# Steps reordered where the stages of a two-block transformer kernel meet

## The reference

```python
h = rmsnorm(x, g_pre_mix);  proj = h @ w_in          # u | x,B,C | q,k,v | f | 3 gates
y_a = s5_mixer(u, ...);  y_b = B * conv3(C * x);  y_c = forgetting_attention(q, k, v, f)
merged = sum(sigmoid(gate_b + bias_b) * (y_b @ w_branch_b) for b in 3 branches)
x = x + rmsnorm(merged @ w_out, g_post_mix)
x = x + rmsnorm(relu(rmsnorm(x, g_pre_mlp) @ w_ff1) ** 2 @ w_ff2, g_post_mlp)
```

```python
h = rmsnorm(x, norm1_g);  proj = h @ w_in_2          # q,k,v of 3 dilations | u,v | 2 gates
merged = sigmoid(gate_a) * (attn @ w_proj_attn) + sigmoid(gate_b) * (sgu @ w_proj_sgu)
x = x + merged @ w_out_2
h = rmsnorm(x, norm2_g);  x = x + (silu(h @ w_ffn_gate) * (h @ w_ffn_up)) @ w_ffn_down
out = rmsnorm(x, final_g)
```

## Time and profile before

| | before |
|---|---|
| median of 3 runs, us | 3589.28 (3587.01 to 3590.35) |
| the profiled execution, us | 3586.24 |
| its span, us | 3584.4 |
| TensorE busy, us (share) | 3479.1 (97%) |
| VectorE busy | 1387.6 (39%) |
| GpSimd busy | 967.8 (27%) |
| ScalarE busy | 941.1 (26%) |
| mean granted TensorE clock, of full | 0.989 |

### The profile page before, as it was taken

One profiled execution on the slowest core, in us unless ns is written; L12 is line 12 of the kernel. 1 busy time (PEld: TensorE's weight loads), 2 busy tenths in 40 slices (PEclk: granted clock), 3 DMA queues, 4 the chain that ended last, 5 costly groups with the idle time before them and its releaser, 6 DMA issues.

```text
span 3584.4 us, 44185 instructions
## 1 busy us (share of the span) xinstructions
PE 3479.1 (97%) x17275; PEld 2873.2 (80%) x17275; DVE 1387.6 (39%) x2452; ACT 941.1 (26%) x1575; POOL 967.8 (27%) x421
## 2 busy tenths in 40 slices
PE   7899999999999999999999999998999999999999
PEld 6688877888877888888778888887788888888887
DVE  6883443123335333333643444335124312232234
ACT  4223434322242111111433333332322211111112
POOL 1552102232215333333212222221322132222321
PEclk9999999999999999999999999999999999999999
DMA  4233012212312111111221212213123111111111
GB/s 131 62 76 95 22 54 65 70 53 65 123 53 83 47 48 56 48 47 47 71 86 47 66 53 59 78 42 115 53 65 111 36 60 52 47 47 47 47 47 59
DMA packets 203976, 226.83 MB, mean 63 GB/s; under 512 B 19224, under 2 KB 177604, under 8 KB 203340
## 3 DMA queue, kind: packets, MB, share of 16 engines
q1 hardware_dynamic: 178556, 169.85, 15.4%
q10 hardware_dynamic: 20912, 44.54, 3.6%
q0 software_dynamic: 4384, 10.74, 0.9%
HBM read 191.30 MB, written 31.69 MB: 62 GB/s over the span
## 4 chain that ended last, share of the span: by engine, by line
PE 87%; DVE 4%; issue 4%; ACT 2%; POOL 1%; DMA 1%; ACTq 0%; DVEq 0%; POOLq 0%
PE ps L274 18%; PE ps L319 16%; PE ps L301 13%; PE ps L302 13%; PE ps L295 13%; PE ps L770 4%; PE ps L2838 2%; PE ps L2809 1%; POOL wlo L266 1%; PE ps L2826 1%; PE ps L2321 1%; PE ps L336 1%; PE ps L510 1%; ACT whi L258 1%; PE ps L2302 1%
## 5 line engine op out<-in xcount | busy, mean ns | idle before, releaser
L266 POOL TENSOR_TENSOR wlo<-raw,whi 128x2048 fp32r<-128x2048 f32 (+1 forms) x162 | 699.4, 4318 | 1731.1 <-ACT whi L258 1730.2
L301 PE MATMUL ps<-h_lo,whi 128*128 128x512 f32 x1856 | 723.8, 390 | 2.0 <-POOL wlo L266 2.0
L302 PE MATMUL ps<-h_hi,wlo 128*128 128x512 f32 x1856 | 723.5, 390 | 0.0
L258 ACT ACTIVATE whi<-raw 128x2048 fp32r<-128x2048 f32 (+1 forms) x162 | 288.1, 1779 | 883.1 <-PE ps L295 595.9
L295 PE MATMUL ps<-h_hi,whi 128*128 128x512 f32 x1856 | 461.6, 391 | 5.0 <-issue 2.7
L295 PEld LDWEIGHTS ps<-h_hi,whi 128*128 128x128 f32 x1856 | 349.2, 188 | 79.0 <-issue 5.8
L301 PEld LDWEIGHTS ps<-h_lo,whi 128*128 128x128 f32 x1856 | 349.5, 188 | 75.7 <-POOL wlo L266 3.1
L302 PEld LDWEIGHTS ps<-h_hi,wlo 128*128 128x128 f32 x1856 | 349.3, 188 | 72.6
L1157 DVE TENSOR_TENSOR big<-big,ps 128x512 f32<-128x512 f32 x400 | 274.4, 687 | 240.3 <-PE ps L274 240.2
L319 PE MATMUL ps<-h_lo,whi 128*128 128x512 f32 x880 | 352.2, 400 | 2.0 <-POOL wlo L266 1.9
L319 PE MATMUL ps<-h_hi,wlo 128*128 128x512 f32 x880 | 344.8, 392 | 0.0
(11 more groups left out here) (335 smaller groups left out, 4817.8 us busy)
## 6 DMA issues: line engine op xcount, KB each, us to landing
raw<-in_w_ff_dram SPq DMA_DIRECT2D x32, 1024.0 KB, 5.2
raw<-in_w_in_dram SPq DMA_DIRECT2D x57, 512.0 KB, 4.6
raw<-in_w_in_dram SPq DMA_DIRECT2D x28, 1024.0 KB, 5.3
raw<-in_w_ffn_gate_dram SPq DMA_DIRECT2D x11, 1024.0 KB, 5.3
raw<-in_w_ffn_up_dram SPq DMA_DIRECT2D x11, 1024.0 KB, 5.3
raw<-in_w_ffn_down_dram SPq DMA_DIRECT2D x11, 1024.0 KB, 4.9
yt<-y_keep ACTq DMA_DIRECT2D x20, 512.0 KB, 3.9
raw<-in_w_out_dram SPq DMA_DIRECT2D x8, 1024.0 KB, 5.0
```

Of the source, the lines that this page charges most:

```text
L258: nc.scalar.activation(whi[c % 2][:, 0:cols], raw[c % 2][:, 0:cols], ACT.Copy).then_inc(s_hi.sem, 1)
L266: nc.gpsimd.tensor_tensor(wlo[c % 2][:, 0:cols], raw[c % 2][:, 0:cols], whi[c % 2][:, 0:cols].bitcast(F32), ALU.subtract).then_inc(s_lo.se ...
L301: nc.tensor.matmul(ps[:, bank + n, :], w(0, k, m * P, P), src[1][:, k, sl], start=False, stop=False)
L302: last = nc.tensor.matmul(ps[:, bank + n, :], w(1, k, m * P, P), src[0][:, k, sl], start=False, stop=k == ks - 1)
```

## The change

Nothing is computed otherwise but for the squarings of S5; steps are put at other places, and each engine's part of a stage is changed to fit.

- *First norm (Start).* ScalarE issues the loads of x pairs 2 and 3 after pair 0 has landed. All four stood first before.
- *Output projections (Out).* `turn` of features 0 to 7 of half 0 stands behind tiles (2,6), (2,7), (3,4) and (3,5), two at each, in place of (2,4) to (2,7). The hi split of the feed-forward's first unit stands amid the features of half 0, that of its second ahead of the features of half 1.
- *Merges.* The first branch's quarters of y are loaded at once, the last two into `gate`, on two more semaphores, and the split of the first branch unit is put ahead of y's. In the loop, the split of the next branch unit stands behind the sigmoids and the split of the next gate unit; it stood ahead of the sigmoids.
- *Feed-forward's last pair.* `dve_norm` ahead of `dve_post`; features 0 to 3 of half 0 ahead of the last rows' sums and of the unit split on ScalarE; turns behind parts 13 and 15 of pass 0 and parts 12 and 13 of pass 1.
- *S5's first round.* VectorE makes round 0's last doubling itself (`first_half`); `taps` ahead of the kernel rows and `by_b(0, 0)` ahead of the scans; a squaring takes four operations in place of six; TensorE does round 1's first two half tiles ahead of `outputs(0)`.
- *Dilated attention's first pass.* `features` ahead of the exponentials.
- *Gate stage.* The eleven loads of `wsp`, `lng`, `lnb` and `bsp` go from ScalarE's queue to SyncE's, behind the first two units.

```diff
-                for q in range(4):
+                def load(q):
                     e.dma_start(big[:, 2 * q:2 * q + 2, :],
                                 A["x"][0, 2 * q * P:(2 * q + 2) * P, :].rearrange("(t p) d -> p t d", p=P)
                                 ).then_inc(x_pair[q].sem, 16)
+                load(0)
+                load(1)
                 e.wait_ge(eps_set.sem, 1)
                 nc.scalar.activation(nst[:, RP, 0:1], eps_c[:, :], ACT.Sqrt)
                 r = self.rows
+                e.wait_ge(x_pair[0].sem, 16)
+                load(2)
+                load(3)
                 for t in range(8):
                     r.act_pre(e, t)
...
                     if g == 0:
-                        self.rows.act_features(e, 0)
-                        split_hi(e, unit_no(self.u + 4))
+                        for k in range(8):
+                            if k == 4:
+                                split_hi(e, unit_no(self.u + 4))
+                            self.rows.act_hi(e, 0, k)
                 if self.gain is not None:
                     e.wait_ge(x_rows.sem, self.rows.x + 8)
                     e.dma_start(scratch["x_keep"], big[:, :, :]).then_inc(d_out.sem, 16)
+                split_hi(e, unit_no(self.u + 5))
...
                                 e.wait_ge(dve_a.sem, self.da + t + 1)
                             tile(j, t, t == 0 if j == 2 else t == 4)
-                            if g == 1 and j == 2:
-                                for k in range(2 * t - 8, 2 * t - 6):
-                                    self.rows.turn(e, 0, k)
+                            k = {(2, 6): 0, (2, 7): 2, (3, 4): 4, (3, 5): 6}.get((j, t))
+                            if k is not None:
+                                self.rows.turn(e, 0, k)
+                                self.rows.turn(e, 0, k + 1)
...
-                self.i = (d_in.take(32 * nb), d_in2.take(32 * nb))
+                self.i = (d_in.take(32 * nb - 16), d_in2.take(32 * nb - 16))
+                self.i2, self.i3 = d_tab.take(16), d_gain.take(16)
...
+            def place(b, k):
+                return gate[:, 2 * k - 4:2 * k - 2, :].rearrange("p a n -> p (a n)") if b == 0 and k >= 2 else yt[:, k % 2, :]
+            def wait_y(self, e, b, k):
+                if b == 0 and k >= 2:
+                    e.wait_ge((d_tab, d_gain)[k % 2].sem, (self.i2, self.i3)[k % 2] + 16)
+                else:
+                    e.wait_ge((d_in, d_in2)[k % 2].sem, self.i[k % 2] + 16 * ((4 * b + k) // 2 + (1 if b == 0 else 0)))
...
             def act(self, e):
                 self.begin(e)
+                for k in range(4):
+                    e.dma_start(self.place(0, k), scratch["y_keep"][0, :, k, :]).then_inc((d_in, d_in2, d_tab, d_gain)[k].sem, 16)
+                split_hi(e, unit_no(self.u + 1))
+                for k in range(4):
+                    self.wait_y(e, 0, k)
+                    nc.scalar.activation(y_hi[:, k, :], self.place(0, k), ACT.Copy).then_inc(ac.sem, 1)
+                def gates(b, i):
...
+                    split_hi(e, unit_no(self.u + 8 * b + 2, i))
                 for b in range(self.nb):
-                    for k in range(4):
-                        n = 4 * b + k
-                        if n >= 2:
-                            e.wait_ge(dve_a.sem, self.lo + n - 1)
-                        e.dma_start(yt[:, k % 2, :], scratch["y_keep"][b, :, k, :]).then_inc((d_in, d_in2)[k % 2].sem, 16)
-                        if k == 0:
-                            continue
-                        if k == 1 and b:
-                            e.wait_ge(pe_b.sem, self.b + 16 * b)
-                        for kk in (0, 1) if k == 1 else (k,):
-                            e.wait_ge((d_in, d_in2)[kk % 2].sem, self.i[kk % 2] + 16 * ((4 * b + kk) // 2 + 1))
-                            nc.scalar.activation(y_hi[:, kk, :], yt[:, kk % 2, :], ACT.Copy).then_inc(ac.sem, 1)
-                    with e.Fori(0, 4) as i:
-                        if self.bias is not None:
-                            e.wait_ge(act_a.sem, 4 * i + (self.aa + 16 * b))
...
-                        split_hi(e, unit_no(self.u + 8 * b + 1, i))
-                        for n in range(4):
...
-                        split_hi(e, unit_no(self.u + 8 * b + 2, i))
+                    if b:
+                        for k in range(4):
+                            e.wait_ge(dve_a.sem, self.lo + (4 * b + k - 1 if b > 1 or k > 1 else 4))
+                            e.dma_start(yt[:, k % 2, :], scratch["y_keep"][b, :, k, :]).then_inc((d_in, d_in2)[k % 2].sem, 16)
+                            if k == 0:
+                                continue
+                            if k == 1:
+                                e.wait_ge(pe_b.sem, self.b + 16 * b)
+                            for kk in (0, 1) if k == 1 else (k,):
+                                self.wait_y(e, b, kk)
+                                nc.scalar.activation(y_hi[:, kk, :], yt[:, kk % 2, :], ACT.Copy).then_inc(ac.sem, 1)
+                    else:
+                        e.wait_ge(dve_a.sem, self.lo + 4)
+                    if b:
+                        split_hi(e, unit_no(self.u + 8 * b + 1))
+                    with e.Fori(0, 3) as i:
+                        gates(b, i)
+                        split_hi(e, unit_no(self.u + 8 * b + 3, i))
+                    gates(b, 3)
...
-                        nc.vector.tensor_tensor(y_lo[:, k, :], yt[:, k % 2, :], y_hi[:, k, :].bitcast(F32),
+                        nc.vector.tensor_tensor(y_lo[:, k, :], self.place(b, k), y_hi[:, k, :].bitcast(F32),
...
                 e.dma_start(gpb[:, :], self.gain.partition_broadcast(P)).then_inc(d_gain.sem, 16)
                 def ups(c, i, us):
-                    split_hi(e, (us[0][0] + 1,) + us[0][1:])
+                    if not (i is None and c == 0):
+                        split_hi(e, (us[0][0] + 1,) + us[0][1:])
                     for n in range(4):
                         if not (i is None and c == 0):
...
                         summed(t)
                         r.act_post(e, t)
-                        if t:
+                        if 0 < t < 5:
                             r.act_pre(e, t - 1)
+                    r.act_pre(e, 4)
+                    for k in range(2):
+                        r.act_hi(e, 0, k)
                     r.act_pre(e, 5)
+                    for k in range(2, 4):
+                        r.act_hi(e, 0, k)
                     e.wait_ge(q_loaded.sem, self.ql + 16)
                     split_hi(e, (v[0] + 1,) + v[1:])
-                    r.act_features(e, 0)
+                    for k in range(4, 8):
+                        r.act_hi(e, 0, k)
                     for t in (6, 7):
                         summed(t)
                         r.act_post(e, t)
...
+                            r.dve_norm(e, t - 2)
                         if t:
                             r.dve_post(e, t - 1)
-                        if t >= 2:
-                            r.dve_norm(e, t - 2)
                     r.dve_post(e, 5)
+                    r.dve_lo(e, 0, 0)
+                    r.dve_lo(e, 0, 1)
                     e.wait_ge(s_begun.sem, upto_unit(v, 1))
                     r.dve_norm(e, 4)
-                    r.dve_lo(e, 0, 0)
-                    r.dve_lo(e, 0, 1)
+                    r.dve_lo(e, 0, 2)
+                    r.dve_lo(e, 0, 3)
                     r.dve_norm(e, 5)
-                    for k in range(2, 8):
-                        r.dve_lo(e, 0, k)
+                    r.dve_lo(e, 0, 4)
+                    r.dve_lo(e, 0, 5)
                     sums(6)
+                    r.dve_lo(e, 0, 6)
+                    r.dve_lo(e, 0, 7)
                     sums(7)
...
                         free(t)
                         part(t, 0)
+                        if t % 2:
+                            turns(t - 13)
                     for t in range(12, 16):
                         part(t, 1)
-                        turns(2 * (t - 12))
+                        if t < 14:
+                            turns(2 * t - 20)
...
                 def half_tables(f):
                     gr = slice(f * GB, f * GB + GB)
-                    e.wait_ge(m["s5_half"], f + 1)
+                    e.wait_ge(m["s5_half"], f)
...
                 for f in range(4):
                     if f == 0:
                         split(f, 1)
-                    half_tables(f)
                     if f:
+                        half_tables(f)
                         split(f, 1)
                         second_powers(f)
                     split(f, 2)
...
                 for j in range(6):
-                    cmul(MR[:, j + 1, :], MI[:, j + 1, :], MR[:, j, :], MI[:, j, :], MR[:, j, :], MI[:, j, :], S[17])
+                    tt(MR[:, j + 1, :], MR[:, j, :], MR[:, j, :], ALU.mult)
+                    tt(S[17], MI[:, j, :], MI[:, j, :], ALU.mult)
```

(63 more changed lines are left out.)

14 lines of the change are left out of this document (2 added, 12 removed).

## The result

The changed kernel takes 3546.77 us (median of 4 runs, 3545.87 to 3549.83), where the kernel before takes 3588.95 in the runs beside it: a ratio of 0.9883, with a 95% interval of 0.9871 to 0.9895. The forecast was 3550, and 3538 to 3562 for its own case. The profiled execution took 3545.9, 1.8 of it outside the span.

The account below looks back on a forecast made before the run. TensorE, busy 3479.1 of 3584.4 us, was taken as the bound, leaving gaps and low clock. Terms 0.4 - 4.3 + 2.9 + 9 + 8.8 + 4.2 + 4 + 5.4 + 8.8 = 39.2 gave median 3550; range 3532 to 3567.

Parts of the forecast that it names:

- its own case: Whole kernel: the forecast's summed gains hold, median 3550 us, between 3538 and 3562; chance 0.56.
- VectorE's part: S5's first round: VectorE's savings and added costs sum to 3.9 us later, states ending some 3 us later.
- the wait for TZ: S5's first round: TZ transfers, no longer covered by the taps, cost VectorE another 3.6 us before the states.
- the contention: S5's first round: VectorE and GpSimd taking turns cost VectorE 9.5 us in place of 8.1, 1.4 more.
- The step of the sum that failed: S5's first round: GpSimd's split of unit (1,1), landing 0.2 us before TensorE needed it, delays TensorE; round -4.3.
- lost cover: S5's first round: gelu and turned y of group 0 lose cover, about 1.3 + 2.3 us, inside the split's wait.
- the whole sum would be 6 us lower: S5's first round: if VectorE and GpSimd shared bandwidth evenly, states end about 1.7 us earlier, whole sum 6 lower.
- rival (d): Merges' loop: the later branch split delays TensorE each turn; a whole split, 6.5 us, costs 130: 3680; chance 0.02.
- The new gap at the eighth normed row: First output projection: the eighth normed row comes late, a new gap of 1.85 us, half the time with low clock (0.9).
- The fourth norm: Feed-forward's last pair: norm before post takes 0.9 us off the fourth normed row.
- one trap: Feed-forward's last pair: a norm meeting GpSimd's split took 3.04 us, not 0.75; it now starts about 0.3 before.
- rival (a): Whole kernel: new waits of 2 us and low clock keep about half; 17 us less gained, 3567; chance 0.22.

Follow-up runs that it names:

- e12: Changed kernel with GpSimd's split of unit (1,1) in S5 held until VectorE has made MM of round 1: 3547.18 us.
- e3: Changed kernel with VectorE's norm of row 5 in the feed-forward's last pair moved ahead of h_lo 2 and 3: 3543.75 us.
- e7: Changed kernel with ScalarE's split of the last unit moved behind h_hi 4 and 5 in the feed-forward's last pair, VectorE's order kept: 3544.45 us.

## Why the prediction was right, and where it was not

*First norm: 0.4, measured nothing.* Where TensorE's last wait of the first norm ends, near 27.9, the two traces differ by 0.03. Over all profiled executions the first turn moves by 1 us, more than the edit could show.

*S5's first round: -4.3, measured -0.7 in one trace, -2.8 by the medians; the wrong reason.* VectorE's part held: the wait for TZ was put at 3.6 and is 4.0, the contention is there, the outputs start at 138.15 in place of 135.63, 2.5 later where 3.9 was worked out.

```profile
135.50 0.07 DVE L1817 MEMSET PP<- 128x16 f32 x1 [4.00 <-DMA TZ<-PP]
```

The step of the sum that failed is "what comes next in order is GpSimd's half tables and then its split of unit (1,1), which landed ... 0.2 us before TensorE needed it". A round has twelve half tiles (not six), four to a unit: the half tiles 1,0 to 1,3 read unit (1,0), and unit (1,1) is first used in the half tile that starts at 163, 10 us later (e12). What is left without that step: 2.5 later, 5.4 of matmuls filled in, 1.2 + 2.1 of lost cover, so 0.4 lost; and then the clock, up to half of a low stretch of 6.8, which comes in most executions and not in all. That the part came out as a loss, as forecast, is luck: the reason given for it was not there, and two that were not given took its place. (Where that passage says that "the whole sum would be 6 us lower", it is the time that would be, not the gain.) I had put the lost cover "inside that same wait" and no low clock behind it. I had not seen either that the half tiles would wait for `by_b(0, 0)` (the 6.6 for `cacc`): it costs nothing, since TensorE still waits 3.0 for `PP` behind them.

*Merges: 2.9 and 9, measured 3.2 and 11.1.* In the second the sequence of the prediction is in the trace, but its terms were shorter: GpSimd's split begins 3.9 us after ScalarE's first load (2469.83), where 5 was said, and holds VectorE for 4.6 as said; the first subtraction, begun within it, takes 3.96, the three behind it 1.21 each. So the last `y_lo` was ready after 13.0 us and not 14.5:

```profile
2473.72 4.62 POOL L266 TENSOR_TENSOR wlo<-raw,whi 128x2048 fp32r<-128x2048 f32 x1 [12.56 <-ACT whi L258]
...
2475.47 5.09 DVE L935 TENSOR_TENSOR y_lo<-yt,y_hi 128x1024 fp32r<-128x1024 f32 x2 [15.35 <-ACT y_hi L880]
2480.49 2.35 DVE L935 TENSOR_TENSOR y_lo<-gate,y_hi 128x1024 fp32r<-128x1024 f32 x2
```

A gap of 0.31 stayed where I had 1.7, and no low clock. The loop's shift cost nothing (between the first turn of the loop and its last the two traces keep their distance to 0.01 us, in both merges): rival (d) is out.

*Output projections: 8.8 and 4.2, measured 10.9 and 4.5.* The new gap at the eighth normed row was named; it is 0.95 and not 1.85, and the clock, which I had fall half of the time, stayed up behind it: VectorE's product of row 5 began 1.1 earlier than I had it.

*Feed-forward's last pair: 4, measured -0.4.* The fourth norm came as worked out (0.8 earlier, 0.9 said), the turns behind it 0.6 to 0.7 later than I had them: by my own figures that norm ended at 1765.0, and I had the turns at 1764.4. The "one trap" was seen and put into rival (a) at 4 us, because the norm would start "0.3 before that split". It started 0.05 after: 4.3 longer, then a gap of 3.81 and 6.8 us of low clock. The price was about right (4 said; e3, which removes it, is 5.6 lower by the traces and 3.0 by the medians), but it was left out of the sum: a margin of 0.3 us, worked out over chains whose other steps came 0.6 us off, is no reason to put such a term at nothing. The Trainium skill, SBUF — State Buffer (Who interferes with whom), says that the order of issue decides who blocks, and that copies and `tensor_scalar` in their fast modes take the shared pair; the 5.05 beside 0.76 in e7 agrees.

*Dilated attention's first pass: 5.4, measured 5.3.*

*Gate stage: 8.8, measured 6.4.* The gap of 7.64 and its low clock went, as said. The gap before the second mix was to grow from 1.5 to 2.9 and grew to 3.8 (0.9 more), with 3.4 of low clock behind it (1.7), which the sum didn't have. The failed step is the 2.5 us counted as gained from the low clock, of which the sum kept 1.1 after the gap's growth, and the clock behind the grown gap, put at nothing. VectorE's chain of 24.5 from the mask to the first `SG` is the same in both (2448.57 to 2473.09, 2422.28 to 2446.80), so a TensorE that runs faster after the mask only comes to it sooner. Here the low clock ended in a wait for another engine and was hidden already, so its end gains nothing. The feed-forward's last pair shows the same: in the changed kernel 3.4 us of low clock lie ahead of turn 2, which waits 0.60; in e7's execution there is none, and it waits 2.21 and comes at the same place within 0.02 us.

*The range.* 3532 to 3567 held, and the forecast's case with it. That it holds to 1 us is in part luck: two errors of 4 us had opposite signs; the largest terms, 20 us from the merges and projections, were right in kind and size.

## What to carry to other kernels

Where an engine is 97% busy, list its gaps and price each with the low clock behind it; then, for each gap filled, work out the chain that is late next, for there the gain is cut. A gain in clock counts only up to the next wait, and a low stretch costs nothing where it lies in a gap. When two engines come to something that only one can hold within a few tenths of a microsecond of each other, put the full price of the worse order into the sum, or move one of them by an instruction, as e3 did for 3.0 us by the medians and 5.6 by the traces.

## What the runs showed that I had not expected

The clock behind the same pair of short gaps (1.2 and 2.1 us) fell in seven of nine executions and not in the two others. That it is the larger part of the scatter of the changed kernel, 3545.9 to 3549.8, is likely but not shown, since only one of its four runs was profiled; one profile can't tell which is usual.

And a queue's issues can be slowed beside another queue's: ScalarE's three loads of the last pair took 3.60 us to issue while SyncE issued its table loads, where they took 2.17 in the kernel before, with that queue idle. It is the third load that grows. In all thirteen profiled kernels with the table loads on SyncE it took 2.3 to 2.7 us; in the three earlier passes of each, and in the kernel before, 1.0 to 1.5.

```profile
2405.50 3.60 ACTq L2480 DMA_DIRECT2D XC<-dil_keep  x3
```
